# Expert weight tiles with neighbouring rows on one partition, and turned operands that take strided columns

## What is computed

```python
def swiglu(h, wg, wu, wd):
    return jnp.einsum('...f,fd->...d', jax.nn.silu(h @ wg) * (h @ wu), wd)

# first mixture: 8 experts, 1024 x 2816, the two best of each token
for e in range(N_EXPERTS):
    out = out + dense_gate[:, e:e + 1] * swiglu(ht, wg[e], wu[e], wd[e])

# second mixture: 4 groups of 4 experts, 1024 x 256, one group of each token, two experts in it
a = jnp.einsum('td,edf->tef', ht, w_gate)
u = jnp.einsum('td,edf->tef', ht, w_up)
hid = jax.nn.silu(a) * u * combine[..., None].astype(ht.dtype)
out = jnp.einsum('tef,efd->td', hid, w_down)
```

## Time and profile before

| | us |
|---|---|
| median of 3 runs | 1628.16 (1625.53 to 1629.66) |
| the profiled execution, own time | 1627.02 |
| its span, first to last instruction | 1625.3 |
| TensorE busy | 1571.9 (97%) |
| VectorE (DVE) busy | 1261.2 (78%) |
| ScalarE (ACT) busy | 1015.4 (62%) |
| transfers of weights issued by SP | 74.1% of 16 DMA engines' span |

### The profile page before, as it was taken

The page is one execution under the profiler, slowest core; times in us unless marked ns, Lnnn a source line. Parts: engine busy times, 40 slices in busy tenths (PEclk is TensorE's granted clock), DMA queues, the critical chain, the costliest instruction groups (busy, mean ns, idle before and its releaser), DMA issues.

```text
span 1625.3 us, 23325 instructions
## 1 busy us (share of the span) xinstructions
PE 1571.9 (97%) x9200; PEld 1379.1 (85%) x9200; DVE 1261.2 (78%) x1111; ACT 1015.4 (62%) x888; POOL 63.8 (4%) x81
## 2 busy tenths in 40 slices
PE   9999999999899999999999999998989999999998
PEld 8979999898788788888878888786879989889986
DVE  6985444599788888888888888888876764778886
ACT  4663444455577777777777777776654454457763
POOL 4000000000100000000000000002000000000010
PEclk9999999999999999999999999999999999989999
DMA  9635555543498999999999999999976435559990
GB/s 275 231 104 194 182 190 190 167 141 104 156 373 304 390 390 338 389 345 389 342 394 384 351 387 344 389 350 391 392 261 195 153 107 169 179 188 353 363 372 27
DMA packets 244795, 444.66 MB, mean 274 GB/s; under 512 B 12116, under 2 KB 122224, under 8 KB 244720
## 3 DMA queue, kind: packets, MB, share of 16 engines
q1 hardware_dynamic: 239488, 426.17, 74.1%
q0 software_dynamic: 3744, 13.12, 2.3%
q10 hardware_dynamic: 1488, 4.34, 0.8%
HBM read 436.52 MB, written 7.09 MB: 273 GB/s over the span
## 4 chain that ended last, share of the span: by engine, by line
PE 73%; DMA 8%; DVE 8%; issue 6%; ACT 5%; POOL 0%; DVEq 0%; ACTq 0%; SPq 0%; POOLq 0%
PE PS L1210 22%; PE PS L1212 21%; PE PS L1211 21%; DMA ring<-in_moe_wu_dram 5%; DVE w_low L1762 3%; ACT w_high L920 3%; PE PS L1299 2%; DMA ring<-in_moe_wd_dram 1%; DMA work<-h_rows_kept,row_no 1%; DVE h L1787 1%; PE PS L1509 1%; PE PS L1428 1%; DVE hT_low L1762 1%; ACT w_high L753 0%; DVE work L1929 0%
## 5 line engine op out<-in xcount | busy, mean ns | idle before, releaser
L1762 DVE TENSOR_TENSOR w_low<-ring,w_high 128x2048 fp32r<-128x2048 f32 (+1 forms) x403 | 919.2, 2287 | 248.2 <-ACT w_high L753 129.8
L920 ACT ACTIVATE w_high<-ring 128x2048 fp32r<-128x2048 f32 x306 | 585.1, 1917 | 203.2 <-PE PS L1212 164.5
L1210 PE MATMUL PS<-w_high,hT_high 128*128 128x512 f32 (+1 forms) x1184 | 416.0, 351 | 10.4 <-DVE w_low L1762 9.1
L1212 PE MATMUL PS<-w_high,hT_low 128*128 128x512 f32 (+1 forms) x1184 | 410.8, 347 | 0.0
L1211 PE MATMUL PS<-w_low,hT_high 128*128 128x512 f32 (+1 forms) x1184 | 410.6, 347 | 0.0
L753 ACT ACTIVATE w_high<-ring 128x2048 fp32r<-128x2048 f32 (+1 forms) x97 | 183.0, 1893 | 129.3 <-PE PS L1212 119.5
L1210 PEld LDWEIGHTS PS<-w_high,hT_high 128*128 128x128 f32 x1184 | 224.5, 190 | 41.3 <-DVE w_low L1762 12.4
L1212 PEld LDWEIGHTS PS<-w_high,hT_low 128*128 128x128 f32 x1184 | 224.5, 190 | 28.1
L1211 PEld LDWEIGHTS PS<-w_low,hT_high 128*128 128x128 f32 x1184 | 224.7, 190 | 26.5
L1210 PE MATMUL PS<-hT_high,w_high 128*128 128x256 f32 x832 | 240.3, 289 | 3.4 <-DVE hT_low L1762 2.3
L1211 PE MATMUL PS<-hT_low,w_high 128*128 128x256 f32 x832 | 236.2, 284 | 0.0
(11 more groups left out here) (343 smaller groups left out, 1158.3 us busy)
## 6 DMA issues: line engine op xcount, KB each, us to landing
ring<-in_moe_wg_dram SPq DMA_DIRECT2D x88, 1024.0 KB, 10.7
ring<-in_moe_wu_dram SPq DMA_DIRECT2D x88, 1024.0 KB, 10.5
ring<-in_moe_wd_dram SPq DMA_DIRECT2D x80, 1024.0 KB
ring<-in_w_in_dram SPq DMA_DIRECT2D x36, 1024.0 KB, 6.1
ring<-in_w_gate_dram SPq DMA_DIRECT2D x16, 1024.0 KB, 8.2
ring<-in_w_up_dram SPq DMA_DIRECT2D x16, 1024.0 KB, 7.5
ring<-in_w_down_dram SPq DMA_DIRECT2D x16, 1024.0 KB
ring<-in_ffn_wg_dram SPq DMA_DIRECT2D x11, 1024.0 KB, 5.3
```

The source lines that it names most:

```text
L920: act.activation(w_high[:, (s.base + k) % SPLITS, :], slot(w), ACT.Copy).then_inc(s.high_taken, 1)
L1210: mm(o, left_high, right_high, start=first, stop=False, skip_group_check=shared)
L1212: return mm(o, left_low, right_high, start=False, stop=last_one, skip_group_check=shared)
L1762: return tt(out_, whole, part.bitcast(F32), ALU.subtract)
```

## The change

Three things change together, and each engine issues the same instructions in the same order as before; the transfers of weights keep their number, order and bytes.

1. Down tiles of the first mixture: partition p takes the rows 2 p and 2 p + 1 of the tile, which are neighbours in HBM, so one piece of 8 KB in place of two of 4 KB. The first down tile of an expert still comes in two transfers, each of which takes every second row, in pieces of 4 KB.
2. The second mixture: a gate or up tile has eight neighbouring rows on a partition, one piece of 8 KB in place of eight of 1 KB, and a down tile two, 8 KB in place of two of 4 KB.
3. What is multiplied with them must stand in the same order. The chunk f of the features of the second mixture is now every eighth column starting at f (`features`, in `gather_half` and `turn_fetched`), and the turned chunk c of the hidden values is every second column within a block of 256, in both mixtures (`turn_hidden`). The first mixture's features stay contiguous, and so do its gate and up tiles.

```diff
+        def neighbours(w, n):
+
+            return w.rearrange("(p k) n -> p k n", k=n)
+
...
         def load1(i, slot_, kind, j, m):
             if kind == "d":
                 w = expert(A["moe_wd"][0], i)
+                src = neighbours(w[(4 * j + 2 * m) * P:(4 * j + 2 * m + 2) * P, :], 2)
                 if (j, m) == (0, 0):
-                    return [(by2(slot_)[:, c:c + 1, :], kays(w, c, 1)) for c in (1, 0)]
-                return [(by2(slot_), kays(w, 4 * j + 2 * m, 2))]
+                    return [(by2(slot_)[:, c:c + 1, :], src[:, c:c + 1, :]) for c in (1, 0)]
+                return [(by2(slot_), src)]
...
         def load2(i, slot_, kind, j, m):
             w = A[{"g": "w_gate_2", "u": "w_up_2", "d": "w_down_2"}[kind]][0]
-            return [(by2(slot_) if kind == "d" else by8(slot_),
-                     expert(w, i * 4 + (2 * j + m)).rearrange("(k p) n -> p k n", p=P))]
+            of_one = expert(w, i * 4 + (2 * j + m))
+            return [(by2(slot_), neighbours(of_one, 2)) if kind == "d" else (by8(slot_), neighbours(of_one, KC))]
...
+            def features(e, f):
+
+                return slice(f * P, (f + 1) * P) if e.by_k else slice(f, D, KC)
+
             def gather_half(e, s, b):
...
-                        mm(PS[:, 2 * b, c * CAP:(c + 1) * CAP], h[:, t, (4 * b + c) * P:(4 * b + c + 1) * P],
+                        mm(PS[:, 2 * b, c * CAP:(c + 1) * CAP], h[:, t, features(e, 4 * b + c)],
                            pick[:, t, :], start=(t == 0), stop=(t == TT - 1))
...
                     last = nc.tensor.transpose(PS[:, 2 * b, c * CAP:(c + 1) * CAP],
-                                               token_rows[0:CAP, (4 * b + c) * P:(4 * b + c + 1) * P], ident[0:CAP, 0:CAP])
+                                               token_rows[0:CAP, features(e, 4 * b + c)], ident[0:CAP, 0:CAP])
...
                     last = nc.tensor.transpose(PS[:, 6 + j % 2, c * CAP:(c + 1) * CAP],
-                                               wk[2 + j % 2][0:CAP, c * P:(c + 1) * P], ident[0:CAP, 0:CAP])
+                                               wk[2 + j % 2][0:CAP, c // 2 * 256 + c % 2:(c // 2 + 1) * 256:2],
+                                               ident[0:CAP, 0:CAP])
```

## The result

The changed kernel takes **1640.94 us** (median of 4 runs, 1639.80 to 1642.92), the kernel before 1627.03 (4 runs beside them, 1625.53 to 1629.66). The ratio is 1.0085 [1.0067, 1.0103]: 13.9 us slower. The forecast was 1630.2, the range 1618 to 1640.

What follows compares the result with a forecast made beforehand. TensorE, busy 97% of the span, was taken as the bound, with most transfers hidden. From 1627.02 us, - 0.6 (eighth expert) + 2.7 (fetches) + 1.1 (stride of eight) gave 1630.2 us; range 1618 to 1640.

Steps and rivals of the forecast that it cites:

- the stride of two: 208 hidden transposes loading every second column, both mixtures: nothing lost, the low end; a full doubling would be 17 us.
- rival C: Strided transposes cost in full: 1636.1 us with the stride of eight alone, 1653 if both double; chance 0.08.
- Stride of eight: Second mixture's 24 fetched-row transposes and 32 gathers loading every eighth column: 0.6 + 0.5, 1.1 us lost.
- The fetches: Second mixture's three fetches of token rows are slower beside 8 KB packets: 2.7 us lost, at most 4.8.
- The first mixture's pieces: First mixture's 8 KB down tiles save 0.5 us of queue time per expert, hidden by idle DMA: costed at nothing.
- rival A: Faster stream cures TensorE's 10.7 us of waits for late tiles: 1616.3 us, or 1621.7 for half; chance 0.18.
- The claim that a trip would change by under 1 us: First-mixture trip: a span change over 1 us would mean the claim that its transfers are covered is wrong.
- The eighth expert: First mixture's eighth expert: its late second down tile arrives sooner beside GpSimd's reads, 0.6 us gained, ends 0 and 1.3.
- D: 8 KB pieces move slower, deciding from 361 GB/s down; at 300 GB/s the second mixture alone gives 1657 us; chance 0.06.
- E: Transfers are cut into 4 KB packets again, so the time stays at 1628 us; chance 0.05.
- B: All three second-mixture fetches pay 1.6 us, as do end reads of kept rows and copies out: 1635.5 us; chance 0.11.
- The signs: Expected in the changed profile: 203835 packets, about 414 GB/s, low-part waits near 10 us, four hidden transposes still 0.33 us.

Runs made afterwards that it cites:

- hidden_stride: Kernel before with only the hidden turns reading every second column, old pieces, branch for a second pass left out: 1632.94 us, ratio 1.0031.
- features_stride: Kernel before with only the second mixture's features (gathers and fetched rows) reading every eighth column, second-pass branch left out: 1632.21 us, ratio 1.0027.
- gather_stride: Kernel before with only the second mixture's 32 first-trip gathers reading every eighth column, second-pass branch left out: 1631.11 us, ratio 1.0029.
- first_by_dve: Kernel before with the first mixture's 8 KB down tiles, DVE writing the hidden order in both mixtures, all turns contiguous: 1628.25 us, ratio 1.0002.
- turns_only: Kernel before with all the strided turns but the old pieces; changed values sent it into a second pass: 2030.86 us.
- order_by_dve: Changed kernel with DVE writing hidden values in the turned order, so TensorE's hidden turns are contiguous: 1635.41 us, ratio 1.0053 to the kernel before.
- gate_up_as_before: Changed kernel with the second mixture's gate and up tiles in 1 KB pieces and features contiguous again: 1633.79 us, ratio 1.0048 to the kernel before.

## Why the prediction was wrong

**The step that failed** is "For the stride of two I take nothing, the low end, because these are short loads of 96 partitions between products whose weights are loaded ahead." The loads went from 141 to 210 ns, and 28 ns of the 69 are on the path, 5.7 us by the rows and 4.0 to 5.5 by two experiments. The reason given did not hold for them: the four transposes of a group follow each other with no product between, one every 83 ns (0.33 us for four), and the loads of a group are longer together, 0.67 us in place of 0.54. So far as the rows show, the rest of the 69 ns is covered by the loads lying partly beside each other, and not by products. The prediction had noticed how little it takes: rival C decides "from 13 ns on each hidden transpose". The ends were nothing and a doubling, 83 ns each; 28 ns is well inside, and a term of 208 operations should have been taken from the middle and not from an end. With 5.2 us here, 3.7 for the gathers and 1.7 for the fetched turns the forecast would have been 1639.7.

The Trainium skill, SBUF — State Buffer, section "Door 1: The DMA port swizzle", note on cachelines, makes a stride of two fp32 free (two hits in 16 bytes) and penalises a stride of eight. By that rule hidden_stride would have cost nothing and features_stride alone something. The measurement contradicts the first half: loads with strides of 2, 4 and 8 took 210, 210 and 207 ns. The prediction priced the two strides in the rule's order, and that order was false for TensorE's fp32 loads.

**Stride of eight**, "a quarter of the doubling", 1.1 us. The fetched turns were taken at 0.6 and have 0.7 in the rows. The gathers were taken at 0.5; their own length is 1.3 (0.8 of it the stride), and they cost 3.7. "A slower read is partly covered by the slower array" was wrong: at a granted clock of 0.50 the sixteen still took 25 ns more each. What was missing is that these gathers stand in the stretch at 1.2 GHz, and lengthen it, by 6.6 us in gather_stride.

**The fetches**, 2.7 us: right in kind, and near in the total (2.4 to 2.7), but not as worked out. The fetch of the chain takes 9.17 us, a little over the forecast 8.5 to 9, and the third one 8.6; the first one, which the prediction took at 1.0 us lost, took 6.4 us in place of 7.6 and was not waited for. There were two waits, not three, and they grew by 1.0 us in sum, under half of the term. The rest is the later reads of the last trip, 0.5 us, and the clock that can fall behind a wait, by the windows above.

**The first mixture's pieces**, nothing: right. first_by_dve shows it, and the rate of 424 GB/s (414 estimated) ends in a queue that stands longer. The low parts' waits stayed, 9.8 us, and rival A fell as the prediction argued: the stream starts late for a reason that no piece changes. The claim that a trip would change by under 1 us held (0.6), but not for its reason: that 0.6 us is TensorE's own.

**The eighth expert**, 0.6 us gained: not shown. The longest wait is 4.2 us, as before; the gain, if there is one, is too small for these runs.

**The rivals.** C was what happened, in a third shape: not a full doubling (1636.1 or 1653), but a partial one for both strides plus clock. D and E fell with the packets and the 424 GB/s. B's 1635.5 rested on longer fetches and longer reads at the end. Both came (two of the three fetches, and 2.1 us of waiting in place of 1.6 in the last trip), but at 0.5 to 0.9 us each and not 1.6; with all that hangs on them they were a fifth of the loss.

**The signs** it named were well chosen: "more means C" was said of 0.33 us for four turns, and the profile had 0.44.

## What to carry to other kernels

Turning the layout of a stream to make its pieces larger moves a stride into an operand of TensorE, and there it is paid on the path: about 28 ns for each short transpose, whatever the stride's size, against pieces whose gain ended in an idle queue. Before such a change, count the operations that will read with a stride, multiply by something from the middle of the bounds, and ask whether any of the DMA time saved was ever waited for. Where a stage already runs at 1.2 GHz, price an edit there by what the stage's clock does too. Read the return of the clock from the first changed instruction and not in windows at fixed times, and repeat the profile, since the moment of the fall differs between two executions of the same kernel.

## What the runs showed that had not been expected

- TensorE's fp32 loads of 96 x 128 take 141 ns from neighbouring columns and 207 to 210 ns from every second, fourth or eighth.
- The rate of the stream still rises at 8 KB: 424 GB/s, after 349, 391 and 406 at 1, 2 and 4 KB.
- The indirect fetch of 96 rows takes 8.6 to 9.4 us beside 8 KB pieces and 6.9 to 8.3 beside 1 KB ones when it is the second or third of the stage; the first is faster beside 8 KB (6.2 to 7.2 against 7.1 to 9.1 us, turns_only with its 7.1 taken in).
- DVE writes and reads the permuted order at no cost that shows: with order_by_dve a trip is 95.6 us, as before (95.7).
- Strided gathers in a stretch at 1.2 GHz make it longer: full clock is back 11.3 to 13.9 us behind the first of them, and 5.6 to 7.1 us where they are contiguous (eight profiles against nine). The mean granted clocks over all timed runs are less sharp: 0.9845 to 0.9875 with strided gathers, without them 0.9876 to 0.9896, but for gate_up_as_before with 0.9871 (turns_only, with its second pass, left out). **Open** stays why the clock falls at another moment in two executions of one kernel, and why gathers that take 25 ns more each hold its return up by so much more than their own length.
